# SyncE holds 64 page numbers in 32 registers and extracts each by a shift or a mask

## The reference

```
k_past = cache_k[j, page_table].reshape(bs, -1, ATT_HEADS, 2, ATT_DH)
v_past = cache_v[j, page_table].reshape(bs, -1, ATT_HEADS, 2 * ATT_DH)
s_past = einsum('bqhcd,bkhcd->bhcqk', q, k_past) * scale
p = softmax(concatenate([s_past, s_new], axis=-1))
w = p[:, :, 0] - lam * p[:, :, 1]
```

## Time and profile before

| | us |
|---|---|
| runs (3) | 1834.12, 1837.66, 1837.75 |
| median | 1837.66 |
| profiled execution, its own time | 1843.85 |
| span of its profile, first to last instruction | 1842.1 |
| PE busy in the span | 1536.4 |
| mean granted clock of PE | 0.915 |

### The profile page before, as it was taken

The page is one execution under the profiler, slowest core; times in us unless marked ns, Lnnn a source line. Parts: engine busy times, 40 slices in busy tenths (PEclk is TensorE's granted clock), DMA queues, the critical chain, the costliest instruction groups (busy, mean ns, idle before and its releaser), DMA issues. The chain is left out here.

```text
span 1842.1 us, 34660 instructions
## 1 busy us (share of the span) xinstructions
PE 1536.4 (83%) x12742; PEld 1377.6 (75%) x12742; DVE 1022.0 (55%) x2157; ACT 718.1 (39%) x1331; POOL 594.1 (32%) x681
## 2 busy tenths in 40 slices
PE   5998979888688676575877999999999789789895
PEld 5888868767567565363757899999999679578793
DVE  4787333453435444354444577977778542368834
ACT  1665243233233332222132445554445331266613
POOL 1454513111111110010531435444445545235540
PEclk9999999998889897697887999999999889899997
DMA  3221334444544444443101323333243223122221
GB/s 114 74 73 51 100 97 147 143 133 148 159 150 151 131 130 145 136 137 116 56 25 39 84 58 108 105 104 95 62 118 107 72 70 91 35 74 72 62 62 49
DMA packets 282257, 178.75 MB, mean 97 GB/s; under 512 B 18874, under 2 KB 280794, under 8 KB 282088
## 3 DMA queue, kind: packets, MB, share of 16 engines
q1 hardware_dynamic: 282088, 176.53, 32.8%
HBM read 159.62 MB, written 16.86 MB: 96 GB/s over the span
## 5 line engine op out<-in xcount | busy, mean ns | idle before, releaser
L170 POOL TENSOR_TENSOR w_low<-w_raw,w_high 128x256 fp32r<-128x256 f32 x608 | 529.9, 901 | 1146.4 <-ACT w_high L161 1146.2
L161 ACT ACTIVATE w_high<-w_raw 128x1024 fp32r<-128x1024 f32 x152 | 160.2, 1054 | 214.9 <-PE proj_lo L194 83.6
L860 PE MATMUL r<-ident,k_pages 128*128 128x128 f32 x512 | 85.3, 320 | 96.3 <-DMA k_pages<-in_cache_k 94.7
L860 PEld LDWEIGHTS r<-ident,k_pages 128*128 128x128 f32 x512 | 69.7, 165 | 105.3 <-DMA k_pages<-in_cache_k 101.2
L1572 PE MATMUL proj<-xh,w_high 128*128 128x288 f32 x440 | 138.4, 315 | 2.8 <-POOL w_low L170 2.8
L1572 PE MATMUL proj<-xh,w_low 128*128 128x288 f32 x440 | 132.6, 301 | 0.0
L1572 PE MATMUL proj<-xl,w_high 128*128 128x288 f32 x440 | 131.7, 299 | 0.0
L1572 PE MATMUL proj_lo<-xh,w_high 128*128 128x256 f32 x440 | 128.6, 292 | 2.1 <-ACT u L1821 2.1
L1572 PE MATMUL proj_lo<-xl,w_high 128*128 128x256 f32 x440 | 125.6, 286 | 0.0
L1572 PE MATMUL proj_lo<-xh,w_low 128*128 128x256 f32 x440 | 124.8, 284 | 0.0
L1572 PEld LDWEIGHTS proj_lo<-xh,w_high 128*128 128x128 f32 x440 | 84.6, 192 | 12.0 <-issue 9.7
(11 more groups left out here) (432 smaller groups left out, 4522.5 us busy)
## 6 DMA issues: line engine op xcount, KB each, us to landing
k_pages<-in_cache_k SPq DMA_DIRECT2D x256, 128.0 KB, 2.3
v_pages<-in_cache_v SPq DMA_DIRECT2D x256, 128.0 KB, 2.3
w_raw<-in_c_in_w SPq DMA_DIRECT2D x48, 512.0 KB, 4.0
w_raw<-in_a_in_w SPq DMA_DIRECT2D x32, 512.0 KB, 4.0
w_raw<-in_b_in_w SPq DMA_DIRECT2D x32, 512.0 KB, 4.4
w_raw<-in_a_out_w SPq DMA_DIRECT2D x16, 512.0 KB, 4.2
st<-in_state_ssd_h SPq DMA_DIRECT2D x16, 512.0 KB, 5.5
out_ssd_h_sample<-st SPq DMA_DIRECT2D x16, 512.0 KB, 5.4
```

The costliest lines, as they stand in the source:

```text
L161: act.activation(k.wh[par][:], k.raw[par][:], ACT.Copy).then_inc(k.sem["w_hi"], 1)
L170: step = pool.tensor_tensor(k.wl[par][:, tiles, :], k.raw[par][:, tiles, :], k.wh[par][:, tiles, :], ALU.subtract)
L860: t = pe.transpose(r_of(k, "keys", u, n, q)[:, c:c + P], k.kb[half][:, 2 * (q % 2) + g, h * P:(h + 1) * P], k.ident[:])
```

## The change

All 64 numbers are loaded once, when the table has landed and before the first period. Two at a time go into one register, the second multiplied by 128 (`page_pair`); 32 such registers are kept. `page_of` no longer loads: it takes its number out of the pair by a shift right by 7 or by a mask with 127 into a fresh register, and declares its range of 0 to 79. It is called just before each DMA, behind the wait, where the loads stood ahead of the wait.

```diff
+    def page_pair(n):
+        low, high = (sp.value_load(k.table[0:1, n + g:n + g + 1], min_val=0, max_val=79) for g in range(2))
+        both = sp.alloc_register(f"pages{n}")
+        sp.reg_mov(both, low + high * PAGE)
+        return both
+
+    numbers = [page_pair(n) for n in range(0, NB * PAGES, 2)]
+
+    uses = itertools.count()
+
     def page_of(n, g):
-        return sp.value_load(k.table[0:1, n * PAGES + g:n * PAGES + g + 1], min_val=0, max_val=79)
+        both, one = numbers[(n * PAGES + g) // 2], sp.alloc_register(f"page_used{next(uses)}")
+        if g % 2:
+            sp.reg_alu(one, both, 7, ALU.logical_shift_right)
+        else:
+            sp.reg_alu(one, both, PAGE - 1, ALU.bitwise_and)
+        return sp.snap(one, donate=True, min_val=0, max_val=79)
...
     def key_pages(u, n, half, free=None):
 
-        pages = [page_of(n, 4 * half + g) for g in range(4)]
         if free:
             sp.wait_ge(sem["r_done"], B_FILL["r"]["keys", *free, 2 * half + 1] + 1)
         for g in range(4):
-            sp.dma_start(k.kb[half][:, g, :], page(keys, pages[g], u)).then_inc(sem[f"k_landed{half}"], 16)
+            sp.dma_start(k.kb[half][:, g, :], page(keys, page_of(n, 4 * half + g), u)).then_inc(sem[f"k_landed{half}"], 16)
 
     def value_pages(u, d, free=None):
         for b in range(2):
-            pages = [page_of(2 * d + b, g) for g in range(PAGES)]
             if free:
                 sp.wait_ge(sem["x_done"], B_FILL["x"]["values", *free] + 1)
             for g in range(PAGES):
-                sp.dma_start(k.vb[b][:, g, :], page(values, pages[g], u)).then_inc(sem[f"v_landed{b}"], 16)
+                sp.dma_start(k.vb[b][:, g, :], page(values, page_of(2 * d + b, g), u)).then_inc(sem[f"v_landed{b}"], 16)
```

More of the change, by code:

```diff
@@ L16 @@
+import itertools
 import math
```

## The result

| | before | after |
|---|---|---|
| median, us | 1837.7 (1834.12 to 1845.26, 4 runs) | 1730.9 (1723.78 to 1733.82, 4 runs) |
| profiled execution, its own time | 1843.85 | 1729.82 |
| span | 1842.1 | 1728.1 |

The ratio is 0.9383, 95% interval 0.9353 to 0.9413: faster by 6.2%, 106.8 us between the medians and 114.0 between the two profiled executions.

A forecast was written before the change was run, and what follows sets the result against it. The prediction took SP's page issues to bound the attention layer. Gains of 83 and 44 less 4 at the front, 123 us off 1843.85, gave 1720.9, or 1715 us as a median, range 1685 to 1772.

The forecast's parts named there:

- What bounds the kernel: Attention layer: SP's never-empty queue is the bound, at 1.08 us a page, of which the load is 0.55.
- a page of 0.86 us: Rival that SP stays the bound, the check coming again at each use: gain 96, 1742 us; chance 0.10.
- The mask or shift, 0.09 us: Extraction at each page issue on SP: adds 0.09 us (bounds 0 and 0.33), so a page costs 0.62.
- The check: Rival: the load's range check is emitted again at each use, 0.33 us a page; 1742 us, chance 0.10.
- the registers: Rival on the count of registers: a page costs SP 0.93 us, gain 71, 1767 us; chance 0.07.
- Second stretch, gain 83: Twenty periods with projection slots: key waits 59.1 go and clock returns 24; 379.74 to 296.6 us, bounds 59 and 91.
- Third stretch, gain 44: Last unit with its tail: key waits 35.6 go, plus 8, a third of the clock's part; bounds 36 and 60.
- The front, cost 4: Layer's start: 64 loads and 32 pairings, 39 us on SP, delay slots 2 and 4; bounds 1 and 8.
- The sum: 83 + 44 - 4 = 123 us off the profiled 1843.85; less 6.2 to the median, 1715 us.
- the clock does not come back: Rival: short waits for ACT hold the clock down, only key waits go: gain 91, 1747 us; chance 0.16.
- Slower, the DMA engines are the bound: Rival: the 16 DMA engines bind, faster issues only queue up, front's cost on top: 1842 to 1846; chance 0.03.

The follow-up runs named there:

- d1: The changed kernel with an unused load of the number put back at every page: 1920.8 us, ratio 1.0393 to the kernel before.
- d2: The changed kernel with an unused load of the number put back at every 2nd page: 1785.8 us, ratio 0.9680 to the kernel before.
- d4: The changed kernel with an unused load of the number put back at every 4th page: 1746.6 us, ratio 0.9461 to the kernel before.
- keysonly: The changed kernel with value pages loading their numbers at every use again, key pages from registers: 1794.1 us, ratio 0.9753 to before.
- d2split: d2 with the second sequence's value pages issued in the following even period, behind its keys: 1771.2 us, ratio 0.9625 to before.

## Why the prediction was right, and where its terms were off

Forecast 1715 us, measured 1730.9, within the range of 1685 to 1772.

*What bounds the kernel*: shown. Taking SP's time away freed PE, putting it back (d1) brought back the waits and more. The way the prediction priced a rival was incomplete, though: it set SP's sum of work against PE's, and for a page of 0.86 us it had 315 us for the second stretch and 120 for the third. d2 has 0.87 us a page, and measured 322.7 and 139.4: the chain from PE's turning to SP's next keys was left out.

*The mask or shift, 0.09 us*: measured 0.05 in the mean (0.58 against 0.53 a page): the mask 37 ns and a step as its own instruction, the shift 39 ns more inside an instruction that was there, where the prediction took a register operation of its own for both. The check did not come back and the registers held, so both of those rivals fell.

*Second stretch, gain 83*: measured 80.6. Waits for keys 59.1, as stated; the clock's part 291.2 - 269.8 = 21.4 where 24 was taken, although the granted clock of 0.99 is almost all that there was to regain. The 32.0 us that the prediction worked out for all of it were too many: the share rose by 10 points and PE's busy time fell by 7%. The share is over the whole stretch, waits included.

*Third stretch, gain 44*: measured 40.4, both ended at the last mean squares (158.6 to 118.2). Keys 35.6 and the clock 98.2 - 88.8 = 9.4 (8 was taken) would be 45; other waits of PE grew by 4.3, as those for ACT and for the prompt weights from DVE, of which the rows of before, to set against the last unit's rows above, are:

```profile
PE r L881 <- ACT past_k_feat L1037: 8.7, 4, 3.2
PE r L881 <- DVE p_prompt L1219: 2.5, 1, 2.5
```

That the waits for keys had hidden them is likely, and not shown.

*The front, cost 4*: the step that was most off in proportion. It measured 8.3 us, 76.8 against 68.5. The two late slots were there, with waits of 2.9 and 2.4 us where 1.0 and 2.9 were worked out. Slot 2's load was issued at 255.6 and not 255: the loads began 1.6 us earlier than the 216 taken, but they and the pairings took 41.2 us and not 39, of which 1 us is that a pairing took 103 ns and a step (0.15 and not 0.12). PE came to that slot about 1 us earlier in this execution, and slot 4's load was issued at 272.2 and not 270.4. The other 3 us were not in the prediction at all: behind these gaps the clock was 0.90 and 0.89 (264 to 297 us) where it had been 1.00, with a few us at 1.2 GHz behind each.

*The sum*: on the profiled executions 80.6 + 40.4 - 8.3 = 112.7 and 1.3 us from outside the layer, 114.0, against the forecast 123. That is 9 of the 16 us of the miss. The other 7 came from the step to the median: the profiled execution of before lay 6.2 us over its median, the one after 1.1 under it.

*The rivals*: "the clock does not come back" fell, with 0.99 in the twenty periods; in the last unit it stayed at 0.85, as the third counted for it said. "Slower, the DMA engines are the bound" fell: the second stretch moved 186 GB/s (187 was forecast) and pages landed in 2.5 us for 2.3. The sentence of the Trainium skill that spoke for it (DMA: Bandwidth & Descriptors, Issuing engines are not separate DMA queues, that the sequencer's time to initiate a DMA is "usually small relative to the DMA itself") does not describe this kernel. Here SP's time for a page was 1.08 us beside 2.3 us from issue to landing, and cutting it to 0.58 made the kernel 6.2% faster.

## What to carry to other kernels

The bound was here a queue engine whose list of waits was empty while PE waited for what it issues, and no busy time showed it. Read a DMA wait as a late issue where landings are short, and count the register instructions around each DMA, not only the DMA. Sum the queue's work against the other engine's period, and also follow the longest chain through it, because the sum alone was not enough: in d4's last unit SP's sum of 101 us fitted into 118, and PE still waited 6.6 us for keys. What is moved ahead of a loop needs a stretch in which its engine would have waited; the same 64 loads cost 8 us of the front in one block and nothing in the gaps.

## What the runs showed of the hardware

A stall of PE costs more than its length. In the twenty periods the length of every version without value waits is the change's 299.1 plus the wait for keys plus the extra PE busy time, which is the slower clock (granted 0.99 in the change, 0.95 in d2 and keysonly, 0.89 before, 0.86 in d1): d2 299.1 + 12.0 + 11.4 = 322.5 (measured 322.7), keysonly 299.1 + 18.6 + 12.0 = 329.7 (329.8), before 299.1 + 59.1 + 21.4 = 379.6 (379.7), d1 299.1 + 84.6 + 22.9 = 406.6 (406.6). The extra does not follow the length of the waits: 12.0 us in 6 waits cost 11.4 more, 18.6 in 8 cost 12.0, 59.1 in 10 cost 21.4 and 84.6 in 10 cost 22.9. d2split, with 7.9 us in 4 waits for keys and values, paid 2.2. Their number orders these five better than their length; no run varied the one without the other.

A DMA instruction on SP took 333 ns in the median with its address in registers and 432 ns with a constant one, for a page of the same 128 KB. No run shows why.

A load of one number cost SP 0.55 us in the kernel before and 0.61 us put back into the changed one, between the extraction and the DMA.
